# Half-size block products in twelve of 22 up steps of a two-layer float32 transformer kernel

## The reference, cut to what matters

```python
D_MODEL = 1024; SEQ = 512; DEPTH = 2; D_FF = 2816; CONV_W = 3

def conv_ffn(h, w_up, conv_w, conv_b, w_down):
    S = h.shape[1]
    u = h @ w_up                                   # 1024 x 5632
    up = jnp.pad(u, ((0, 0), (CONV_W - 1, 0), (0, 0)))
    u = conv_b + sum(conv_w[j] * up[:, j:j + S] for j in range(CONV_W))
    gate, val = jnp.split(u, 2, axis=-1)
    return (jax.nn.silu(gate) * val) @ w_down      # 2816 x 1024

for layer in range(DEPTH):
    x = x + attention(rms_norm(x, norm_mix[layer]))
    x = x + conv_ffn(rms_norm(x, norm_ffn[layer]), ...)
```

## Time and profile before

| | us |
|---|---|
| median of 3 runs | 1191.71 (1190.48 to 1192.66) |
| the profiled execution's own time | 1191.57 |
| its span, first to last instruction | 1189.8 |
| up stage of layer one, about | 295 to 534 |
| up stage of layer two, about | 831 to 1070 |

### The profile page before, as it was taken

One profiled execution on the slowest core, in us unless ns is written; L12 is line 12 of the kernel. 1 busy time (PEld: TensorE's weight loads), 2 busy tenths in 40 slices (PEclk: granted clock), 3 DMA queues, 4 the chain that ended last, 5 costly groups with the idle time before them and its releaser, 6 DMA issues.

```text
span 1189.8 us, 18961 instructions
## 1 busy us (share of the span) xinstructions
PE 1174.8 (99%) x6874; PEld 999.6 (84%) x6874; DVE 862.7 (73%) x1502; ACT 617.0 (52%) x1033; POOL 348.5 (29%) x429
## 2 busy tenths in 40 slices
PE   9999999999999999999999999999999999999998
PEld 7768886778888888888999887988888888888998
DVE  6588968945766566579897898855766666579986
ACT  6554337855434333345565789945534334335563
POOL 0633547830042522211000366730042421211000
PEclk9999999999999999999999999999999999999999
DMA  7555352253398785436554110053387574326553
GB/s 281 182 187 199 142 202 65 73 142 106 106 238 238 199 217 184 175 109 211 186 160 138 62 37 2 1 125 107 106 192 179 156 172 130 106 71 208 176 173 127
DMA packets 51555, 174.54 MB, mean 147 GB/s; under 512 B 4720, under 2 KB 6128, under 8 KB 41504
## 3 DMA queue, kind: packets, MB, share of 16 engines
q1 hardware_dynamic: 36352, 127.51, 31.3%
q0 software_dynamic: 15136, 46.14, 16.3%
HBM read 171.50 MB, written 52.47 MB: 188 GB/s over the span
## 4 chain that ended last, share of the span: by engine, by line
PE 93%; DVE 3%; ACT 2%; issue 1%; POOL 0%; DVEq 0%; ACTq 0%; POOLq 0%
PE ps L2554 28%; PE ps L2556 27%; PE ps L2555 27%; PE ps L2269 3%; PE ps L2253 3%; PE ps L2069 1%; PE ps L2520 1%; PE ps L2110 1%; PE ps L2237 1%; PE ps L2140 1%; ACT probs L977 1%; DVE w_lo L1705 1%; DVE xT L1725 0%; PE ps L2121 0%; ACT w_hi L1148 0%
## 5 line engine op out<-in xcount | busy, mean ns | idle before, releaser
L2554 PE MATMUL ps<-h_hi,w_hi 128*128 128x512 f32 x704 | 274.4, 390 | 0.0
L2555 PE MATMUL ps<-h_lo,w_hi 128*128 128x512 f32 x704 | 273.9, 389 | 0.0
L2556 PE MATMUL ps<-h_hi,w_lo 128*128 128x512 f32 x704 | 273.9, 389 | 0.0
L1394 DVE TENSOR_TENSOR w_lo<-raw,w_hi 128x2048 fp32r<-128x2048 f32 (+1 forms) x62 | 123.0, 1984 | 118.3 <-ACT w_hi L887 118.3
L1216 ACT ACTIVATE cv<-u_in,vec 128x512 f32<-128x512 f32 x88 | 71.2, 816 | 180.4 <-DVE u_in L1835 178.3
L887 ACT ACTIVATE w_hi<-raw 128x2048 fp32r<-128x2048 f32 (+1 forms) x72 | 121.8, 1692 | 69.1 <-PE ps L2556 69.1
L2554 PEld LDWEIGHTS ps<-h_hi,w_hi 128*128 128x128 f32 x704 | 132.2, 188 | 27.6 <-issue 0.7
L2556 PEld LDWEIGHTS ps<-h_hi,w_lo 128*128 128x128 f32 x704 | 132.2, 188 | 27.6
L2555 PEld LDWEIGHTS ps<-h_lo,w_hi 128*128 128x128 f32 x704 | 132.2, 188 | 27.3
L762 POOL TENSOR_TENSOR v<-act 128x256 f32<-128x256 f32 x16 | 43.3, 2707 | 345.2 <-DVE act L1872 345.2
L2554 PE MATMUL ps<-a_hi,w_hi 128*128 128x256 f32 (+1 forms) x440 | 138.9, 316 | 2.2 <-DVE a_lo L1709 2.2
(11 more groups left out here) (276 smaller groups left out, 2421.6 us busy)
## 6 DMA issues: line engine op xcount, KB each, us to landing
raw<-in_f_up SPq DMA_DIRECT2D x44, 1024.0 KB, 5.0
w_sums<-in_f_w_down POOLq DMA_DIRECT2D x22, 1024.0 KB, 8.7
w_sums<-in_f_w_down POOLq DMA_DIRECT2D x44, 512.0 KB, 9.0
raw<-w_sums SPq DMA_DIRECT2D x44, 512.0 KB, 4.2
raw<-in_a_in_wide SPq DMA_DIRECT2D x12, 1024.0 KB, 6.1
raw<-in_f_w_down SPq DMA_DIRECT2D x22, 512.0 KB, 3.9
raw<-in_f_w_down SPq DMA_DIRECT2D x22, 256.0 KB, 4.0
bias_tiles<-bias_rows SPq DMA_DIRECT2D x1, 4096.0 KB, 27.0
```

The lines of the kernel that those rows point to most:

```text
L1394: dve.tensor_tensor(w_lo[:, s, 0:n], raw[:, s, 0:n], w_hi[:, s, 0:n].bitcast(F32), ALU.subtract)\
L2554: pe.matmul(dst, s_hi, m_hi, start=start, stop=False)
L2555: pe.matmul(dst, s_hi, m_lo, start=False, stop=False)
L2556: return pe.matmul(dst, s_lo, m_hi, start=False, stop=stop)
```

## The change

Twelve up steps, 5 to 8 of layer one and 2 to 9 of layer two (`SEVENS`), are made as seven half-size products: the weights of a step are a 2 x 2 arrangement of blocks (first or last 512 features by gate or value channels), the features another (first or last 512 features by first or last 256 tokens). The seven products take seven blocks of weights of 512 KB ("units") of which three are plain, and seven blocks of features with 256 tokens, of which three are plain.

- **TensorE**: a changed step is 7 units x 2 channel tiles x 4 feature tiles x 3 = 168 matmuls with 256 columns. A step uses three PSUM banks, (0, 1, 2) and (3, 6, 7) in turn.
- **Weights**: in all up steps but the first, weights are loaded, split and used in units of 512 KB in a ring of four (`raw4`, `hi4`, `lo4`); a plain step takes 4 units, a changed step 7. A load waits until the unit four before it has its lo part.
- **ScalarE** snapshots the partial sums between products (`keep`, four copies of 128x512 a step); **VectorE** adds the rest (`first_row`, `second_row_sum`, `second_row`).
- **Sums of weights**: two scratch tensors in HBM for each layer, `w_two` and `w_more`: per changed step two copies of 1 MB, one accumulating DMA of 1 MB (`two_up`) and two of 512 KB (`three_up`, `four_up`). Layer one's 8 copies stand on GpSimd in attention one, layer two's 16 on SyncE in attention one (`copy_up`). `two_up` of layer two is eight accumulating DMAs of 1 MB, one behind every fourth count of `r_used[1]` in the down stage of layer one. `three_up` and `four_up` of layer two are issued by GpSimd before and in attention two, as are layer two's 11 copies of `w_down`; layer one's 11 copies of `w_down` move to up steps 1 to 3, its 22 `sum_weights` to steps 4 to 9, one for every two units in steps 5 to 8; layer two's 22 stand behind every second unit from step 1.
- **Sums of features**: once a layer ScalarE writes `gained` (8 x 128x512), VectorE makes four sums of 128x1024 (`sums_of_features`) in the step two before the first changed one, ScalarE their hi and, one step later, VectorE their lo (`sum_lo`, 4 x 128x1024).
- The loops over the up steps are written out.

```diff
+SEVENS = ((5, 6, 7, 8), (2, 3, 4, 5, 6, 7, 8, 9))
...
+                for m, (i, j) in enumerate(UP_UNITS[l]):
+                    r = m % 4
+                    sp.wait_ge(w_lo_done, U_UP[l] + (1 + m // 2 if m < 4 else m - 1))
...
+            def two_up(l, z):
...
+                pool.dma_start(w_two[l][z], f_up[l, SEVENS[l][z], 1], accum_op=ALU.add, max_dma_last_dim=8192)\
+                    .then_inc(up_sums, 16)
...
+                for k in range(4, FT - 4):
+                    behind(0, *UP_UNITS[0][unit_of(0, 5) + 2 * (k - 4)])
+                    sum_weights(0, k)
...
+                for z in range(len(SEVENS[1])):
+                    pool.wait_ge(r_used[1], 4 * z + 3)
+                    two_up(1, z)
...
+                for k in range(FT):
+                    behind(1, *UP_UNITS[1][2 * k])
...
+                if u % 2 == 0 and 2 <= u < 2 + 2 * len(SEVENS[1]):
+                    four_up(1, u // 2 - 1)
+                elif u % 2 and u >= 3:
+                    copy_weights(1, (u - 3) // 2)
...
+                    if i == SEVENS[l][0] - 2:
+                        sums_of_features(l, 0)
+                        sums_of_features(l, 1)
+                    if i == SEVENS[l][0] - 1:
+                        for j in range(4):
+                            sum_lo(l, j)
...
+                    for j, (b, moving) in enumerate(((0, 0), (2, 3), (0, 4), (1, 1), (0, 5), (2, 2), (0, 6))):
+                        m = unit_of(l, i, j)
+                        r = m % 4
+                        pe.wait_ge(w_lo_done, U_UP[l] + 2 + m + 1)
...
+                        if j in (2, 4, 5, 6):
+                            pe.wait_ge(f_snap, LANDED + SNAP_AT[l][i] + {2: 1, 4: 3, 5: 2, 6: 4}[j])
```

More of the change, by code:

```diff
@@ new lines, in second_row_sum, with second_row @@
+                def second_row_sum(i):
+                    dve.wait_ge(f_snap, LANDED + SNAP_AT[l][i] + 4)
+                    x = u_in[:, 2:4, 2 + HS:2 + S]
+                    dve.tensor_tensor(x, x, both(kept[:, 1]), ALU.add).then_inc(f_in, 1)
+                def second_row(i):
+                    bank = seven_banks(l, i)[0]
+                    minus = [rbc_minus[:, t * HS:(t + 1) * HS].unsqueeze(1).to_broadcast([P, 2, HS]) for t in range(2)]
+                    dve.wait_ge(f_done, DONE_AT[l][i] + 7)
+                    dve.wait_ge(f_t0, 2 * FT * l + 4 * (i - 1) + 4)
+                    dve.tensor_tensor(u_in[:, 2:4, 2:2 + HS], both(ps[:, bank, :]), minus[0], ALU.mult).then_inc(f_in, 1)
+                    dve.wait_ge(f_in, IN_AT[l][i] + 2)
+                    x = u_in[:, 2:4, 2 + HS:2 + S]
+                    dve.tensor_tensor(x, x, minus[1], ALU.mult).then_inc(f_in, 1)
@@ L1868, in ffn_step, with seven_step @@
                         seven_lo(l, 1, 1)
-                    dve.wait_ge(f_t0, 2 * FT * l + 4 * i + 4)
-                    for q in range(2):
-                        dve.wait_ge(f_silu, FT * l + 2 * i + q + 1)
-                        dve.tensor_tensor(act[:, 2 * i + q, :], cv[:, q, :], cv[:, 2 + q, :], ALU.mult)\
-                            .then_inc(f_act, 1)
-                    if not last:
-                        lo(U_UP[l] + 2 * i + 3, SLOT, 1)
-                ffn_step(0, first=True)
-                with dve.Fori(1, UP_STEPS - 1) as i:
-                    ffn_step(i)
-                ffn_step(UP_STEPS - 1, last=True)
+                    gated(i)
+                    if i < UP_STEPS - 1:
+                        unit_lo(l, m + 6)
+                        unit_lo(l, m + 7)
+                def seven_step(i):
+                    m, behind = unit_of(l, i), i - 1 in SEVENS[l]
+                    if behind:
+                        second_row(i - 1)
+                        unit_lo(l, m + 3)
+                        taps(i - 1, (0, 1))
+                    unit_lo(l, m + 4)
+                    if behind:
+                        taps(i - 1, (2, 3))
+                    unit_lo(l, m + 5)
+                    first_row(i, 0)
+                    if behind:
+                        gated(i - 1)
+                    unit_lo(l, m + 6)
+                    second_row_sum(i)
+                    unit_lo(l, m + 7)
+                    unit_lo(l, m + 8)
+                    first_row(i, 1)
+                    unit_lo(l, m + 9)
+                unit_lo(l, 0)
+                unit_lo(l, 1)
+                chain.then_wait(dve.memset(u_in[:, :, 0:2], 0.0))
+                dve.wait_ge(rbc_ok, l + 1)
+                for i in range(UP_STEPS):
+                    if i in SEVENS[l]:
+                        seven_step(i)
+                    else:
+                        plain_step(i)
             first_attention()
@@ L2426, in feed_forward @@
                             ins.then_inc(f_done, 1)
-                channels(0, 2, True, sums=True)
-                channels(0, 3, True, roots=True)
-                with pe.Fori(1, UP_STEPS) as i:
-                    for q in range(4):
-                        channels(i, q, False)
+                channels(0, 2)
+                channels(0, 3)
+                for i in range(1, UP_STEPS):
+                    if i in SEVENS[l]:
+                        seven_step(i)
+                    else:
+                        for q in range(4):
+                            channels(i, q)
             attention(0)
```

437 lines of the change are left out of this document (347 added, 90 removed).

## The result

The changed kernel takes 1207.12 us (median; 1206.18 to 1208.82) where the kernel before takes 1192.01: a ratio of 1.013, 95% interval 1.0113 to 1.0148. It is slower by 15 us; 1187.6 had been forecast and a range to 1203. The profiled execution took 1206.97 us, its span is 1205.2.

What follows compares the result with a forecast made beforehand. TensorE, 99% busy, was taken as the bound. Against the profiled 1191.57 us, -19.2 + 13.2 + 1.0 + 0.5 + 0.5 = -4.0 gave 1187.6 us; the forecast's own range was 1183 to 1192, the full range 1177 to 1203.

Steps and rivals of the forecast that it cites:

- twelve steps on TensorE: Up stages: a changed step takes 20.16 us on TensorE instead of 21.76, saving 1.60 each, 19.2 us for twelve.
- four waits on entering: Entries to the changed steps: VectorE's w_lo is late by 0.3, 4.7, 3.8 and 4.8 us, less 0.4: 13.2 us.
- exits from the changed steps: Plain steps behind a run: VectorE's leftovers of 10.2 us end before its next input at 10.9, so no cost.
- DMA in changed steps: Loads and sum_weights take 19.8 of 20.16 us in a changed step and just fit; 1.0 us for all such waits.
- down stage one, accumulations: Layer one's down stage: two_up accumulations beside unit loads cost 0.5 us, between 0 and 10.
- attention two: GpSimd issues 19 more DMAs of 0.56 us each there; 0.5 us, between 0 and 10.6.
- attention one: SyncE's 16 copies of 1 MB could delay one load of bias tiles by some 3 us; taken as 0.
- VectorE inside the run: In a changed step VectorE has some 18.8 us of work against 20.16, so TensorE does not wait for it.
- The exit needs nothing: Claim that leaving a run of changed steps costs 0: VectorE's 10.2 us of leftovers end before its input at 10.9.
- a rival of 0.17: DMA becomes the bound in 9.5 changed steps once a load takes over about 7 us: +15 us, 1202.8; chance 0.17.
- Two of the prediction's signs: Changed steps: no ScalarE waits on DMA beside sum_weights and none on snapshots were forecast; waits for raw would show it wrong.
- the down stage's rival: Large accumulations starve the down stage's loads: +10 us, 1197; chance 0.08.

Runs made afterwards that it cites:

- e9: e1's order, four changed steps in each layer, layer two's GpSimd work in a written order (6 accumulations beside changed steps): 1183.58 us, 0.9919 of the kernel before.
- e11: As e9, but with the changed kernel's order of sums of features and their lo parts on VectorE: 1198.48 us, ratio 1.0055 to the kernel before.
- e12: As e9, but layer two's 22 accumulations on w_down's sums stand behind every second unit, 14 beside changed steps, not 6: 1186.38 us.
- e1: The changed kernel with only VectorE's order in the two steps before the first changed one altered, twelve changed steps kept: 1193.97 us, 1.0013 of the kernel before.
- e13: As e1, but GpSimd's sums of activations for pairs 3 to 10 are replaced by one fill per pair in both layers: 1183.84 us.
- e8: As e1, but the 44 accumulating DMAs on w_down's sums move 8 columns of every 512: 1190.95 us, one run.
- e6: e1's order, four changed steps in layer two, sums of activations spread, layer one's 1 MB accumulations and layer two's w_down copies moved to up steps: 1188.58 us.
- e2: The changed kernel with layer two's GpSimd sums of activations for pairs 3 to 10 held until the last up step's activations are there: 1209.23 us.
- e3: The changed kernel with three DMA placements altered: bias tiles before copies, layer one's 1 MB accumulations in up step one, layer two's w_down copies on SyncE: 1211.80 us.

## Why the prediction was wrong, by its own steps

| step | predicted | the traces |
|---|---|---|
| twelve steps on TensorE | -19.2 | -20.3, a step takes 20.07 us |
| four waits on entering | +13.2 | +13.1 (0.3, 4.8, 3.5, 4.8, less 0.4) |
| half clock at three of them | none | +5.5 (2.1, 1.6, 1.9) |
| exits from the changed steps | 0 | +1.4 in layer one, +7.0 in layer two (2.5 of it clock) |
| DMA in changed steps | +1.0 | +1.2 |
| down stage one, accumulations | +0.5 | +2.1, in some runs 0 |
| attention two | +0.5 | +1.7; -0.3 to +3.5 in e9, e11 and e12, one and the same code |
| attention one | 0 | +1.8; 0.1 to 1.1 in the same three |
| output projection of layer one | not seen | +1.6 |

The right-hand column adds up to 15.1, the traces differ by 15.4. Its waits are gaps between starts of matmuls, less the usual spacing, and so 0.1 to 0.2 us longer than in the lists. Of the 19.5 us between 1187.6 and the result 8.4 are the exits and 5.5 the clock.

**TensorE's gain** was right and 1.1 us larger than forecast, since the spacing is 119.4 ns and not 120. **VectorE inside the run** was right too: it is busy 56.6 us in three changed steps (433.7 to 493.9), 18.9 a step, where 18.8 had been worked out. So was the **entry**: four waits at the four named places, with sizes to 0.3 us. e1 and e11 show that the order makes them, all but the last: in layer two's step 2 the one other order that was tried leaves 4.7 us too. What failed there is that the sum stopped at the wait. The kernel before had already shown, in a stretch that I didn't look at, what can follow: behind a gap of 1.75 us at 662 to 663 stands this window (mean clock 0.64):

```profile
664.30:667.50 3.20, 3.20 (x15) 0.64 0.21 46
```

The three long waits of the entries cost their length and some 40% more.

**"The exit needs nothing"** is the step that failed. It put the exits at nothing: it counted VectorE's operations by durations from the earlier trace rows, where GpSimd stands still beside every tap (its one set of sums runs from 343.7 to 347.9), and did not ask what GpSimd does in step 10. Measured, the exits cost 8.4 us. `gate_sums` is in the change: its wait for the last changed step is one line, and it turns one set of sums per step into seven sets in a row. e13 prices GpSimd's sums of pairs 3 to 10 in both layers at 10 us with twelve changed steps, against e1.

**DMA** was forecast as just fitting, with a rival of 0.17 where it doesn't. It just fits: the page's list of issues has (KB each, median us to landing)

```profile
raw<-in_f_up SPq DMA_DIRECT2D x68, 512.0 KB, 6.6
...
raw<-w_two SPq DMA_DIRECT2D x24, 512.0 KB, 7.1
raw<-w_more SPq DMA_DIRECT2D x24, 512.0 KB, 6.9
```

the rival's limit was 7. In layer two's changed steps the medians are 7.3 to 7.5, over that limit, and TensorE lost 1.2 us and not 15: the rival had the limit too low. Two of the prediction's signs did come, waits of ScalarE for `raw` (26.5 us from 905 to 1040) and a wait for a snapshot, and they meant little. The prediction's price for loads was read from the earlier trace rows, where packets of 2 and 4 KB are mixed; it holds for 4 KB, since in e8 the loads beside changed steps move 23.0 MB in 57.3% of 125 us, 321 GB/s. The Trainium skill's rule ("DMA: Bandwidth & Descriptors", "Queues, rings and completion order") that engines take packets from their queues in turn, by which the loads would get 185 GB/s of 182 needed (an estimate, which takes the trace's packets for the skill's), agrees with loads that just arrive in time; no run here separates it from a mere sharing of the time. This rival's time, 1202.8, was the nearest to the result, and its cause was not the result's.

**Down stage one and attention two** were in their bounds and above the value taken; attention one had no bounds, it was put at nothing. How much of the two attention blocks' 3.5 us the change makes is open, since they vary by as much without an edit. The output projection's late load was not thought of, though it is the mechanism of the down stage's rival: a large accumulation, a load behind it.

## What to carry to other kernels

When a change makes the bound engine's work denser, lay out the steps in which it starts and ends, not only the steady ones: here the steady steps gave all that was promised, and the edges took 27 us where the steps brought 20. At an edge, price the other engines' operations with the durations that they have beside each other, and put work that is due later behind what the bound engine waits for next: the order of eight operations a layer was worth 15 us. A saving that fills the last idle time of a helper engine may be worth less than half of it taken: with the better order in both, twelve changed steps are 2 us slower than the kernel before (e1), and eight with plain steps around them and a written order of GpSimd's work are 10 us faster (e9).

## What the runs showed of the hardware

- GpSimd's sums of 128x256 float32 slow VectorE's two-operand work while they run: taps of 128x512 from 747 to 1222 ns, `w_lo` of 128x1024 from 1.22 to 1.76 us, `g_lo` from 0.69 to 1.22 us. The delay falls on either side: in the kernel before, GpSimd's first sum of a step starts at 343.66 beside a `w_lo` of 128x2048, and takes 2.71 us where the next one takes 0.73, while `w_lo` keeps its 2.28. A fill on GpSimd in their place (e13) left the taps at 747 ns, and `u_in`, whose one input is in PSUM, kept its 678 ns beside the sums. This is what the Trainium skill says ("SBUF — State Buffer", "Who interferes with whom"): an instruction of VectorE with two inputs in SBUF contends with one of GpSimd that reads SBUF, not with one that only writes it. The runs agree.
- TensorE's granted clock fell to 0.50 for 3.4 to 10.2 us at a time at 22 of the 23 gaps between matmul starts of 3.7 us or more in the profiled runs (not at one of 3.8 in e6): during the gap, within 0.5 us behind it, or, where a gap of 2.5 us stood just ahead, up to 0.6 us before it. It also fell behind some gaps of 1.75 to 2.9 us: the same gap of 2.2 us at the entry of layer one's down stage was followed by a stretch of 3.4 us in e1 and e9, and by none in the changed kernel and in e2. What decides between them was not found.
- DMAs of GpSimd that wait for one another stop all that stands behind them on GpSimd: one accumulation 3.6 us late in e3 cost TensorE 1.9 us and a stretch at half clock in a stage without any load of its own at the limit.
